# Token factors and gate columns by way of device memory, and the rotation table turned as one tile

## What is computed

```python
h = rms_norm(x, pre_norm_g)                    # one factor per token: rsqrt(mean(x*x) + eps)
proj = einsum('bsd,dc->bsc', h, w_in)          # 1024 x 4616
aq, ak, av, az, mq, mk, mv, mo, mz, mi, mf = split_columns(proj)
ya = moba_attention(partial_rope(aq, pos), partial_rope(ak, pos), av)   # cos, sin: a table of 512 x 32
...
qk = silu(causal_depthwise_conv(concat(mq, mk), conv_w, conv_b))
lf = log_sigmoid(mf + f_bias)                  # per token and head; ig = mi + i_bias
bcum = cumsum(lf)
D = where(causal, bcum[t] - bcum[s] + ig[s], -inf)
m_t = max(bcum + m, max_s(D))
s = (q @ k.T) * exp(D - m_t)
nq = ... + sum(s)
hm = num / max(abs(nq), exp(-m_t))
...
y = concat(ya, ym) @ w_out
out = x + rms_norm(y, post_norm_g)
```

## Time and profile before

| what | us |
|---|---|
| median of 3 runs | 318.51 (318.29 to 319.93) |
| the profiled execution: its span, first to last instruction | 316.2 |
| what lies around the span, taken from the median | 2.3 |
| PE busy | 309.4 (98%) |
| DVE busy | 225.4 (71%) |
| ACT busy | 165.2 (52%) |
| POOL busy | 95.9 (30%) |

### The profile page before, as it was taken

How to read it: one execution, slowest core, us unless ns; L and a number is a source line. 1 busy time by engine, 2 the same in 40 slices (tenths; PEclk the granted TensorE clock), 3 DMA queues, 4 the chain that set the end, 5 groups by cost and what they waited for, 6 DMA issues and landing times.

```text
span 316.2 us, 4992 instructions
## 1 busy us (share of the span) xinstructions
PE 309.4 (98%) x1599; PEld 256.4 (81%) x1599; DVE 225.4 (71%) x508; ACT 165.2 (52%) x336; POOL 95.9 (30%) x118
## 2 busy tenths in 40 slices
PE   8999999999999999999999999999999999999992
PEld 4888888888888888888888888778888888888882
DVE  2544999748998699968998568964577766856534
ACT  3548857287345324663157563384556876353301
POOL 8201006056350213002320025592711984000000
PEclk9999999999999999999999999999999999999999
DMA  7941553956725486645864332210220473310111
GB/s 222 323 99 38 153 149 93 170 163 150 134 68 146 134 158 205 188 124 122 180 227 151 102 90 77 73 66 31 67 68 0 125 200 145 133 68 0 68 66 67
DMA packets 29081, 38.30 MB, mean 121 GB/s; under 512 B 3624, under 2 KB 15184, under 8 KB 29056
## 3 DMA queue, kind: packets, MB, share of 16 engines
q1 hardware_dynamic: 27424, 34.51, 36.2%
q0 software_dynamic: 1472, 3.34, 7.0%
q10 hardware_dynamic: 160, 0.14, 0.1%
HBM read 33.68 MB, written 4.29 MB: 120 GB/s over the span
## 4 chain that ended last, share of the span: by engine, by line
PE 93%; issue 3%; DMA 2%; DVE 0%; DVEq 0%; SPq 0%; ACT 0%; POOLq 0%; POOL 0%; ACTq 0%
PE bank L1476 24%; PE bank L1478 24%; PE bank L1477 24%; PE bank L1814 3%; PE bank L1524 3%; PE bank L1758 3%; PE bank L1779 3%; PE bank L1612 2%; DMA farena<-in_x 2%; PE bank L1708 1%; PE bank L1505 1%; PE bank L1769 1%; PE bank L1613 1%; PE bank L1552 1%; PE bank L1551 1%
## 5 line engine op out<-in xcount | busy, mean ns | idle before, releaser
L778 ACT ACTIVATE w_hi<-w_raw 128x512 fp32r<-128x512 f32 x71 | 43.7, 626 | 63.2 <-PE bank L1478 51.1
L1476 PE MATMUL bank<-w_hi,xT_hi 128*128 128x512 f32 (+1 forms) x180 | 72.5, 403 | 0.0
L1478 PE MATMUL bank<-w_hi,xT_lo 128*128 128x512 f32 (+1 forms) x180 | 69.8, 388 | 0.0
L1477 PE MATMUL bank<-w_lo,xT_hi 128*128 128x512 f32 (+1 forms) x180 | 69.3, 385 | 0.0
L1043 DVE TENSOR_TENSOR w_lo<-w_raw,w_hi 128x512 fp32r<-128x512 f32 x64 | 45.5, 721 | 11.1 <-ACT w_hi L778 11.0
L1476 PE MATMUL bank<-xT_hi,w_hi 128*128 128x512 f32 x128 | 50.8, 397 | 0.0
L1478 PE MATMUL bank<-xT_hi,w_lo 128*128 128x512 f32 x128 | 50.1, 392 | 0.0
L1477 PE MATMUL bank<-xT_lo,w_hi 128*128 128x512 f32 x128 | 50.0, 390 | 0.0
L1478 PEld LDWEIGHTS bank<-w_hi,xT_lo 128*128 128x128 f32 x180 | 33.8, 188 | 7.2
L1476 PEld LDWEIGHTS bank<-w_hi,xT_hi 128*128 128x128 f32 x180 | 33.9, 188 | 5.8 <-issue 0.4
L1477 PEld LDWEIGHTS bank<-w_lo,xT_hi 128*128 128x128 f32 x180 | 34.0, 189 | 5.5
(11 more groups left out here) (211 smaller groups left out, 581.8 us busy)
## 6 DMA issues: line engine op xcount, KB each, us to landing
w_raw<-in_w_in SPq DMA_DIRECT2D x72, 256.0 KB, 2.9
w_raw<-in_w_out SPq DMA_DIRECT2D x16, 256.0 KB, 2.7
kq_rows<-stage SPq DMA_DIRECT2D x8, 256.0 KB
gy<-kq_rows SPq DMA_DIRECT2D x8, 256.0 KB, 3.5
gy<-in_x SPq DMA_DIRECT2D x4, 512.0 KB, 5.4
out_y<-gy SPq DMA_DIRECT2D x7, 256.0 KB, 2.1
farena<-in_x SPq DMA_DIRECT2D x4, 256.0 KB, 5.3
farena<-in_x SPq DMA_DIRECT2D x2, 512.0 KB, 7.5
```

The lines of the kernel that those rows point to most:

```text
L778: a.activation(hi, raw, ACT.Copy).then_inc(w_hi_done, 1)
L1476: pe.matmul(o, hi, m_hi, start=start, stop=False)
L1477: pe.matmul(o, hi, m_lo, start=False, stop=False)
L1478: return pe.matmul(o, lo, m_hi, start=False, stop=stop)
```

## The change

- `rx_rows` goes, and DVE's copy of the bank. POOL sends `rx` to device memory as a row of 512 (a piece of 4 bytes per token), waits for it, and reads the row back to all 128 partitions of `rbc`. DVE and the convolution now wait for that transfer. DVE's multiplication that ends in `gate_sb` is moved behind the cuts of slots 10 and 11 and the four low parts of `mv`.
- `gate_cols` goes, and the copy to `aT`. SP, behind its load of slot 22, waits for the gate rows and sends them to device memory (five transfers); behind its load of slot 24 it waits for these and reads 32 rows of 128 back as 32 columns (`gate_col`), again in pieces of 4 bytes, 4096 of them. ACT's `emt` and `decays` use that tile and wait for it.
- `rope_rows` makes one turn of 128 columns instead of four of 32. The result has 128 rows of 128, and POOL sends it to device memory by four transfers instead of one.

```diff
+            g.wait_ge(rx_done, 1)
+                g.dma_start(rx_dram.rearrange("o (t p) -> p (o t)", p=P), rx[:]).then_inc(rx_out, 16)
+            g.wait_ge(rx_out, 16)
+            g.dma_start(rbc[:], rx_dram.to_broadcast([P, SEQ])).then_inc(rbc_done, 16)
...
-            v.wait_ge(rbc_ps, 1)
-            v.tensor_copy(rbc[:], bank[5][:]).then_inc(rbc_done, 1)
-            v.wait_ge(rbc_done, 1)
...
             link(v.tensor_tensor(gate_rows, bank[7][0:P // 2, :], gate_low_rows, ALU.add))
-            v.tensor_tensor(gate_rows, gate_rows, rbc[0:P // 2, :], ALU.mult).then_inc(gate_sb, 1)
             cut(RING + 2)
             cut(RING + 3)
             for t in range(NT):
                 mv_low(t)
+            v.wait_ge(rbc_done, 16)
+            v.tensor_tensor(gate_rows, gate_rows, rbc[0:P // 2, :], ALU.mult).then_inc(gate_sb, 1)
...
+                if n == COLS_OUT:
+                    sp.wait_ge(gdiff_done, 1)
+                    sp.wait_ge(gneg_done, 1)
+                    for j in range(NT):
+                        rows_of_tile = slice(MH * j, MH * (j + 1))
+                        sp.dma_start(col_dram[rows_of_tile, :], gate_rows[rows_of_tile, j * P:(j + 1) * P])\
+                            .then_inc(cols_out, 16)
+                    sp.dma_start(col_dram[NT * MH:, :].rearrange("(h j) p -> h (j p)", j=NT), gate_rows[32:32 + MH, :])\
+                        .then_inc(cols_out, 16)
+                if n == COLS_BACK:
+                    sp.wait_ge(cols_out, 16 * (NT + 1))
+                        sp.dma_start(gate_col[:], col_dram.rearrange("g p -> p g")).then_inc(cols_back, 16)
...
-                a.activation(decay[j], decay[j], ACT.Exp, bias=aT[:, j, 4 * j + h:4 * j + h + 1])\
+                a.activation(decay[j], decay[j], ACT.Exp, bias=gate_col[:, NT * j + h:NT * j + h + 1])\
...
-                    a.wait_ge(aT_done, 1)
+                    a.wait_ge(cols_back, 16)
...
-                if b == S_QK + 6:
-                    v.wait_ge(gcol_ps, 1)
-                    v.tensor_copy(aT[:], bank[7][:].rearrange("p (t c) -> p t c", t=NT)[:, :, 0:16])\
-                        .then_inc(aT_done, 1)
...
-                for t in range(NT):
-                    mm = pe.transpose(bank[6][0:2 * ROT, t * P:(t + 1) * P], rope_sb[:, t, :], ident[:])
-                mm.then_inc(rope_ps, 1)
+                pe.transpose(bank[6][:, 0:P], rope_sb[:].rearrange("p t c -> p (t c)"), ident[:]).then_inc(rope_ps, 1)
...
-                    elif n == 1:
-                        pe.wait_ge(rbc_done, 1)
```

More of the change, by code:

```diff
@@ L89 @@
 NU = NT * AH
+COLS_OUT, COLS_BACK = 22, 24
 UNITS = [("mv", t) for t in range(NT)]
@@ L255, in build @@
         wg = sb("wg", [P, NK, P], F32R)
-        aT = sb("aT", [P, NT, 16])
-        emt = sb("emt", [P, NT, MH])
+        gate_col = sb("gate_col", [P, 2 * NT * MH])
+        emt = sb("emt", [P, MH, NT])
         ssx = sb("ssx", [P, NT])
@@ L314, in build @@
         rope_t = [f_part(F_COS, SEQ), f_part(F_SIN, SEQ)]
-        rope_flat = f_part(F_SIN, SEQ)[0:2 * ROT, :]
+        rope_flat = f_part(F_SIN, P)
         def by_block_order(ap):
@@ L360, in build @@
         g_dram = nc.dram_tensor("g_rows", (16, SEQ), F32, kind="Internal").ap()
+        rx_dram = nc.dram_tensor("rx_row", (1, SEQ), F32, kind="Internal").ap()
+        col_dram = nc.dram_tensor("col_rows", (2 * NT * MH, P), F32, kind="Internal").ap()
         x_in = [sem(f"x_in{c}") for c in range(len(X_CHUNKS))]
@@ L382, in build @@
         rx_done = sem("rx_done")
-        rbc_ps = sem("rbc_ps")
+        rx_out = sem("rx_out")
+        cols_out = sem("cols_out")
         rbc_done = sem("rbc_done")
@@ L402, in build @@
         grows_done = sem("grows_done")
-        gcol_ps = sem("gcol_ps")
-        aT_done = sem("aT_done")
+        cols_back = sem("cols_back")
         emt_done = sem("emt_done")
@@ L550, in _ @@
                     sp.dma_start(wg_raw[:], w_in[0, :, MG:MG + 8].rearrange("(k p) c -> p k c", p=P)).then_inc(wg_in, 16)
+                if n == COLS_OUT:
[9 more added lines that the diff above has]
+                    sp.wait_ge(cols_out, 16 * (NT + 1))
+                    with nc.allow_non_contiguous_dma(reason="a column per row"):
+                        sp.dma_start(gate_col[:], col_dram.rearrange("g p -> p g")).then_inc(cols_back, 16)
                 if n == S_QK + 6:
@@ L639, in _ @@
             rsqrt(rx[:], msx[:]).then_inc(rx_done, 1)
+            g.wait_ge(rx_done, 1)
+            with nc.allow_non_contiguous_dma(reason="one factor per token"):
+                g.dma_start(rx_dram.rearrange("o (t p) -> p (o t)", p=P), rx[:]).then_inc(rx_out, 16)
+            g.wait_ge(rx_out, 16)
+            g.dma_start(rbc[:], rx_dram.to_broadcast([P, SEQ])).then_inc(rbc_done, 16)
             g.wait_ge(gmax_done, 1)
@@ L682, in _ @@
             g.wait_ge(rope_flat_done, 1)
-            g.dma_start(rope_dram.rearrange("q j s -> (q j) s"), rope_flat).then_inc(rope_out, 16)
-            g.wait_ge(rope_out, 16)
+            for t in range(NT):
+                g.dma_start(rope_dram.rearrange("q j s -> (q j) s")[:, t * P:(t + 1) * P],
+                            rope_flat[t * 2 * ROT:(t + 1) * 2 * ROT, :]).then_inc(rope_out, 16)
+            g.wait_ge(rope_out, 16 * NT)
             for q in range(2):
@@ L840, in rope_evac @@
                 a.wait_ge(rope_ps, 1)
-                a.activation(rope_flat, bank[6][0:2 * ROT, :], ACT.Copy).then_inc(rope_flat_done, 1)
+                a.activation(rope_flat, bank[6][:, 0:P], ACT.Copy).then_inc(rope_flat_done, 1)
             def conv_silu(n):
@@ L904, in _ @@
                 if b == ST_AT[0]:
-                    a.wait_ge(aT_done, 1)
-                    a.activation(emt[:], bank[7][:].rearrange("p (t c) -> p t c", t=NT)[:, :, 32:32 + MH],
-                                 ACT.Exp).then_inc(emt_done, 1)
+                    a.wait_ge(cols_back, 16)
+                    a.activation(emt[:].rearrange("p h t -> p (h t)"), gate_col[:, NT * MH:], ACT.Exp)                        .then_inc(emt_done, 1)
                 for h in range(MH):
@@ L1197, in head_stats @@
                     v.bn_stats(bns[:, q, :], pv[:, q, 0:MD])
-                link(v.scalar_tensor_tensor(out=den[:], in0=pv[:, :, MD], scalar=-1.0, in1=emt[:, t0:t0 + 2, h],
+                link(v.scalar_tensor_tensor(out=den[:], in0=pv[:, :, MD], scalar=-1.0, in1=emt[:, h, t0:t0 + 2],
                                             op0=ALU.mult, op1=ALU.max))
@@ L1636, in qk_slot @@
                         pe.wait_ge(xt_lo, NK)
-                    elif n == 1:
-                        pe.wait_ge(rbc_done, 1)
-                    else:
+                    elif n >= 2:
                         pe.wait_ge(u_done, n - 1)
```

8 lines of the change are left out of this document (removed).

## The result

The changed kernel takes 330.67 us (median of 6 runs, 329.77 to 331.63) against 318.4 for before; the ratio is 1.0392, interval 1.0373 to 1.0412. That is 12.3 us slower. Forecast were 324.2, at most 330.5. The profiled execution has a span of 329.1 where before had 316.2, so 12.9 us are to be found in the profiles.

The account below looks back on a forecast made before the run. PE was taken to bound the kernel, without idle time from 46 to 310.6 us. Factors 3.7 plus columns 2.0 gave 5.7 us, the turns' 1.2 swallowed: 318.5 + 5.7 = 324.2 us, range 320.5 to 330.5.

Parts of the forecast that it names:

- Where PE is only just served: At the scores of the first head's second tile, 69.77 us, behind a gapless 3.3 us chain from `emt`.
- The factors' write: POOL's write of `rx` to device memory, taken as 2.7 us to landing, bounds 1.9 and 5.8.
- Late by 3.7: `gate_sb` at 40.0 against ACT's first gate row at 36.33 before, delaying the whole chain behind it by 3.7 us.
- spread: The read of the factors' row back to all partitions of `rbc`, taken as 4.6 us, bounds 3.8 and 5.8.
- The range: Whole kernel: 320.5 to 330.5 us; the main case's own bounds gave 321.7 to 326.3.
- The columns: Gate columns land 3.9 us behind slot 24's load, at 68.45, so `emt` is 2.0 us later still.
- The turns: Eleven PE turns removed ahead of the second tile's scores, 1.2 us, swallowed by PE's wait there.
- The rival in which the covers hold: Factors and columns arrive before ACT needs them, so only the turns count: 317.3 us; chance 0.12.
- PE's wait at the table: PE may wait at the table's turn, `rope_scale` being 3.7 us late; contained in the later wait, adding nothing.
- The clock: Rival: PE's waits, 6.9 us over two places, make the clock fall, costing 1.9 us more: 326.1; chance 0.15.
- Small pieces are dear: Rival: factors' write 3.1 us more, or columns at their upper bound, 2.7 more: 327 to 330 us; chance 0.15.

Follow-up runs that it names:

- e6: The changed kernel with the factors' 512 pieces written 512 bytes apart, and the spread reading an input vector instead: 323.19 us, one run.
- e8: The kernel before with the factors' write to device memory added, which nobody reads: 323.73 us, ratio 1.0185.
- e1: The kernel before with the gate columns through device memory and the table's one turn, factors still by PE's turns: 319.42 us, ratio 1.0039.
- e3: The kernel before with only the table's one turn in place of four, and four transfers of its rows: 318.17 us, ratio 1.0000.
- e10: e9 with ACT's `emt` moved ahead of the cut of slot 23: 321.35 us, ratio 1.0124.
- e9: e1 with the columns' transfers out and back moved ahead of the load of slot 22: 321.76 us, ratio 1.0125.
- e4: The changed kernel with 41 matmuls of ones put ahead of PE's wait for the table: 333.48 us, ratio 1.0487.
- e7: The changed kernel with the factors' write issued from ACT, behind its cuts of slots 8 to 11, instead of POOL: 333.16 us, one run.

## Why the prediction was wrong

- *Where PE is only just served* was right: the scores of the second tile carry the whole 12.8 us, and nothing behind them changed. That everything from `gate_sb` to them stands in series held: 12.0 late at ACT's first gate row, 12.8 at the scores, and the 0.9 between is the columns.
- *The factors' write*, taken as 2.7 us with 5.8 as upper end, is the step that failed. It took 9.5, because its 512 pieces go into one 2 KB stretch (e6: 2.9 with the pieces apart). I bounded it by the writes of whole rows and by a read in many pieces; no row of before had small writes to neighbouring addresses, and a range made of rows of other kinds did not cover it. Late by 3.7 became late by 12.0: 6.8 us of write, 1.0 of spread (5.6 instead of 4.6), and 0.5 because all of this execution up to `rx` ran half a microsecond later.
- *The loads beside the write* were not in the sum at all. In the changed kernel they hide behind the factors' own wait; e8 shows them to be worth 5.2 us alone.
- *The range* was narrower than the rows behind it. The sum is given with upper bounds of 5.0 and 2.8, but the upper bounds worked out above it are 8.0 and 4.7. The 5.0 follows from no row; 2.8 is the slower rate of the pieces without the write. With 8.0 and 4.7 the top would have been 331.2, above what was measured, though by way of a write of 5.8 us that was not the one that came.
- *The columns* were given 2.0 us on top, at least 1.1 or nothing. They added 0.9 in the changed kernel, and in e1, where the factors are on time, 0.7 at the scores. The forecast had them land 3.9 us behind slot 24's load, at 64.55 + 3.9. In e1 that load landed at 63.9 (issued 59.07, 4.8 us) and the columns at 66.7 (issued 62.05, 4.6 us), 2.8 behind it, a little under the 3.1 of the fastest small reads of before. So the pieces were priced nearly rightly by other small reads, and 0.7 of the difference is the load, which came earlier than before. The Trainium skill's rule against a last dimension in pieces (DMA: Bandwidth & Descriptors, Rules for kernel authors) thus bears on the factors' write more than on the columns' read. Its sum of 2.0 us plus the size (same page, Anatomy of one DMA — SWDGE (gpsimd) path) is 7.5 too low for that write, which is on the path that the fit is for. The columns' read was issued by SP, for which the page does not give that fit; it took 2.6 more.
- *The turns* (1.2 us) were swallowed, as forecast; e3, with three of the eleven gone and no small pieces, showed no gain either. The rival in which the covers hold, at 317.3, took all eleven as gained, which no run shows.
- *PE's wait at the table* did not add, as forecast. *The clock* did fall, but the 1.9 us that the rival put on it did not come, since it fell ahead of the second wait. In e6, whose factors came as forecast, it fell behind it and cost 1.7: 3.7 at the scores and 1.7 of the clock give that kernel's 5.3 us of span to 0.1.
- *Small pieces are dear* was the rival that came, beyond its price: 330.67 us, where it had 327 to 330, and by another sum: the write 6.8 us over its term and not 3.1, the columns under theirs.

## What to carry to other kernels

A transfer in small pieces has to be priced for its direction and its neighbours: here small reads could be priced by other small reads, but small writes that meet in one stretch of device memory took three times as long as the same writes apart, and the loads in flight beside them waited as long. Before a few turns on the matrix engine are given for a round through device memory, look for the point where the engine meets the chain that the data is on; a late start of that chain is lost one for one, and turns saved ahead of it may be worth nothing. A slow clock cost only where the engine had no wait left in front of it.

## What was not expected of the hardware

- 512 writes of 4 bytes into one 2 KB stretch took 9.3 to 10.1 us to land from POOL's queue (five kernels) and 9.1 from ACT's (one); the same writes 512 bytes apart took 2.9, and 128 writes of 16 bytes into the same 2 KB 2.8.
- While they last, reads of device memory beside them take 9.9 to 11.5 us for 256 KB where they took 2.7 before.
- 4096 reads of 4 bytes landed in 4.6 us with weight loads alone beside them, and in 9.0 to 10.0 beside a spread of 640 KB (e10, e9).
- The granted clock fell behind an idle stretch of 2.7 us (e4) when PE had already been working again for over 1 us, and behind one of 2.5 us (e7); behind one of 2.9 us (e9) it did not fall. The length of the idle stretch alone does not tell.
